# Logarithms, the first unit pair, the second modulation sums and two pairs of unit buffers moved in a two-block transformer kernel

## The reference, cut to what matters

```
mod = silu(c) @ w_ada + b_ada                 # sh1, sc1, g1, sh2, sc2, g2
h = rms_norm(x) * (1 + sc1) + sh1
z, xbc, dt, q, k, v = split(h @ w_in)
y_ssd = norm(ssd(silu(conv(xbc)), dt) * silu(z))     # 4 chunks of 128 tokens
y_sb: logits = q k^T * scale; log_rem = log_sigmoid(-logits) below the diagonal
      log_between = reversed cumulative sum of log_rem - log_rem
      weights = exp(log_sigmoid(logits) + log_between);  y_sb = weights v
x = x + g1 * (concat(y_ssd, y_sb) @ w_out)
x = x + g2 * swiglu(rms_norm(x) * (1 + sc2) + sh2)
```

## Time and profile before

| what | before |
|---|---|
| time, median of 3 runs | 2187.24 us (2186.93 to 2187.7) |
| profiled execution | 2188.19 us, span 2186.4 us |
| PE busy | 98%, 9964 matmuls |
| DVE busy | 1037.7 us (47%) |
| ACT busy | 750.0 us (34%) |
| POOL busy | 890.1 us (41%) |
| PEld busy | 1685.0 us (77%) |
| mean granted TensorE clock | 0.987 |

### The profile page before, as it was taken

How to read it: one execution, slowest core, us unless ns; L and a number is a source line. 1 busy time by engine, 2 the same in 40 slices (tenths; PEclk the granted TensorE clock), 3 DMA queues, 4 the chain that set the end, 5 groups by cost and what they waited for, 6 DMA issues and landing times.

```text
span 2186.4 us, 26047 instructions
## 1 busy us (share of the span) xinstructions
PE 2131.9 (98%) x9964; PEld 1685.0 (77%) x9964; DVE 1037.7 (47%) x1726; ACT 750.0 (34%) x1106; POOL 890.1 (41%) x717
## 2 busy tenths in 40 slices
PE   7999999999999999999999989999999998999999
PEld 5888888888888445888888867767778876888887
DVE  5445653562434895566256162655655644110111
ACT  4124321222223786322122243543454333222221
POOL 4445545454433211554455334222221243454444
PEclk9999999999999999999999989999999999999999
DMA  4223333422531000342442222111111122223222
GB/s 167 96 97 135 137 118 133 171 101 73 194 115 63 1 1 20 135 153 101 156 148 101 74 92 86 41 56 58 39 58 58 57 79 77 96 77 109 103 75 99
DMA packets 34204, 204.97 MB, mean 94 GB/s; under 512 B 4160, under 2 KB 5312, under 8 KB 14784
## 3 DMA queue, kind: packets, MB, share of 16 engines
q1 hardware_dynamic: 31968, 196.84, 25.6%
q10 hardware_dynamic: 2144, 6.88, 1.0%
HBM read 199.58 MB, written 2.10 MB: 92 GB/s over the span
## 4 chain that ended last, share of the span: by engine, by line
PE 68%; issue 14%; POOL 11%; DVE 4%; ACT 1%; DMA 0%; SPq 0%; POOLq 0%; DVEq 0%; ACTq 0%
PE PS L508 14%; PE PS L509 14%; PE PS L510 14%; POOL WL L446 11%; PE PS L599 4%; PE PS L601 3%; PE PS L600 3%; PE PS L777 2%; PE PS L790 2%; PE PS L808 2%; PE PS L958 1%; PE PS L926 1%; PE PS L920 1%; PE PS L1031 1%; PE PS L899 1%
## 5 line engine op out<-in xcount | busy, mean ns | idle before, releaser
L446 POOL TENSOR_TENSOR WL<-WR,WH 128x512 fp32r<-128x512 f32 (+2 forms) x692 | 858.5, 1271 | 1186.9 <-ACT WH L1152 1186.9
L508 PE MATMUL PS<-Hh,WH 128*128 128x512 f32 x1536 | 606.2, 395 | 22.9 <-DVE Hl L1679 9.8
L509 PE MATMUL PS<-Hl,WH 128*128 128x512 f32 x1536 | 601.3, 391 | 0.0
L510 PE MATMUL PS<-Hh,WL 128*128 128x512 f32 x1536 | 600.9, 391 | 0.0
L1152 ACT ACTIVATE WH<-WR 128x2048 fp32r<-128x2048 f32 (+2 forms) x173 | 305.9, 1768 | 702.3 <-PE PS L510 661.5
L508 PEld LDWEIGHTS PS<-Hh,WH 128*128 128x128 f32 x1536 | 290.6, 189 | 89.2 <-issue 14.6
L509 PEld LDWEIGHTS PS<-Hl,WH 128*128 128x128 f32 x1536 | 290.7, 189 | 62.2 <-issue 2.2
L510 PEld LDWEIGHTS PS<-Hh,WL 128*128 128x128 f32 x1536 | 290.5, 189 | 61.0
L508 PE MATMUL PS<-Gh,WH 128*128 128x512 f32 x592 | 232.2, 392 | 0.0
L509 PE MATMUL PS<-Gl,WH 128*128 128x512 f32 x592 | 232.0, 392 | 0.0
L510 PE MATMUL PS<-Gh,WL 128*128 128x512 f32 x592 | 231.7, 391 | 0.0
(11 more groups left out here) (279 smaller groups left out, 2372.6 us busy)
## 6 DMA issues: line engine op xcount, KB each, us to landing
WR<-wA SPq DMA_DIRECT2D x125, 1024.0 KB, 4.8
AW<-wada SPq DMA_DIRECT2D x24, 1024.0 KB, 6.8
WR<-wB SPq DMA_DIRECT2D x24, 768.0 KB, 4.1
WR<-wC SPq DMA_DIRECT2D x24, 640.0 KB, 3.9
X<-x_in SPq DMA_DIRECT2D x8, 256.0 KB, 6.5
W1K<-w1k ACTq DMA_DIRECT2D x1, 2048.0 KB, 8.0
W1V<-w1v ACTq DMA_DIRECT2D x1, 2048.0 KB, 12.9
out<-X SPq DMA_DIRECT2D x8, 256.0 KB, 4.8
```

Source lines behind the costliest of these rows:

```text
L446: ins = nc.gpsimd.tensor_tensor(WL[:, s, piece], WR[:, s, piece], WH[:, s, piece].bitcast(F32), ALU.subtract)
L508: nc.tensor.matmul(PS[:, b, :], wh[:, c, cols], pe_h, start=c == 0, stop=False)
L509: nc.tensor.matmul(PS[:, b, :], wh[:, c, cols], pe_l, start=False, stop=False)
L510: last = nc.tensor.matmul(PS[:, b, :], wl[:, c, cols], pe_h, start=False, stop=c == seg.chunks - 1)
```

## The change

It has six parts.
1. Own buffers (`WX`) for the high and low parts of the first two units of qkv and of gu2a, at addresses that are free then. Their high parts no longer wait for the tiles of unit u-2. In `dense_squares` ACT writes them before the squares of the last unit's tiles. POOL makes the low part of the first in one 128x2048 instruction (`first_low`), DVE that of the second (`low_of_unit`), in the residual of dn1b ahead of tile 7 and in that of woh ahead of tile 6. With `low_at`, the additions for tile 6 also stand ahead of tile 7.
2. The masks' copies, whose place the new buffers of qkv use, go behind qkv tile 5.
3. Start: ACT calls `hi(1)` behind the third square, and `hi(2)` behind the eighth; POOL signals each of unit 1's four pieces, PE waits piece by piece, and `norm_stats` stands behind unit 1's first tile.
4. `mod_sums(1)` goes from between gu1b and dn1b to the norm behind dn1b: 11 columns ahead of the sum of `ACCF`, 13 behind `norm_stats`, in bank 6. DVE adds its bias behind the norm's chunks.
5. Stick-breaking: ACT's logarithm 1 ahead of exponential 2, DVE's cap 2 ahead of halves 0.
6. Chunks: `low_y(1)` goes from the end of chunk 3 into `last_rows`, behind `gate_y(2)` and a residual tile of wog.

```diff
+        WX = {SEGS["qkv"].unit0: (at("WXH0", 60, [P, KMAX], F32R), at("WXL0", 80, [P, KMAX], F32R)),
+              SEGS["qkv"].unit0 + 1: (at("WXH1", 68, [P, KMAX], F32R), at("WXL1", 88, [P, KMAX], F32R)),
+              SEGS["gu2a"].unit0: (at("WXH2", 64, [P, KMAX], F32R), at("WXL2", 80, [P, KMAX], F32R)),
+              SEGS["gu2a"].unit0 + 1: (at("WXH3", 52, [P, KMAX], F32R), at("WXL3", 88, [P, KMAX], F32R))}
...
+            def first_low(u):
+
+                wh, wl = WX[u]
+                pool.wait_ge(hi_s, u + 1)
+                nc.gpsimd.tensor_tensor(wl[:, :], WR[:, u % 2, :], wh[:, :].bitcast(F32), ALU.subtract)\
+                    .then_inc(lo_s, 1)
...
-                    body(0, 1)
+                    pool.wait_ge(hi_s, 2)
+                    for j in range(4):
+                        piece = slice(j * KMAX // 4, (j + 1) * KMAX // 4)
+                        nc.gpsimd.tensor_tensor(WL[:, 1, piece], WR[:, 1, piece], WH[:, 1, piece].bitcast(F32),
+                                                ALU.subtract).then_inc(w1l_s if j < 3 else lo_s, 1)
...
-                            if stats and first and k == 0 and tiles[0] == 0:
+                            if stats and first and k == (seg.unit0 == 0) and tiles[0] == 0:
                                 norm_stats()
...
-                    if r == 1:
-                        mod_sums(l)
+                    if r == 1 and l == 0:
+                        mod_sums(0, 5, 0, 24)
...
+            mod_sums(1, 6, 0, 11)
             pe.wait_ge(ssf_s, DC)
             nc.tensor.matmul(PS[:, 5, :], ones[:, :], ACCF[:, :], start=True, stop=True).then_inc(meanf_t, 1)
             norm_stats()
+            mod_sums(1, 6, 11, 24)
...
                     act.wait_ge(raw_s[s], 16 * (u // 2 + s))
+                    if u in WX:
+                        nc.scalar.activation(WX[u][0][:, :], WR[:, s, :], ACT.Copy).then_inc(hi_s, 1)
+                        return
                     if u >= 2:
                         act.wait_ge(tile_s, TILES_AFTER[u - 2])
...
-                    if u < seg.units - 1:
+                    ahead = u < seg.units - 1 or seg.unit0 + u + 2 in WX
+                    if ahead:
                         hi(seg.unit0 + u + 2)
...
-            for m in range(DC):
+            for m in range(3):
                 square(m)
             hi(1)
+            for m in range(3, DC):
+                square(m)
+            hi(2)
...
                     logarithm(i5, 0)
+                    logarithm(i5, 1)
                     exponential(i5, 2)
-                    logarithm(i5, 1)
                     logarithm(i5, 2)
...
+            def low_of_unit(u):
+
+                wh, wl = WX[u]
+                dve.wait_ge(hi_s, u + 1)
+                dve.wait_ge(lo_s, u)
+                nc.vector.tensor_tensor(wl[:, :], WR[:, u % 2, :], wh[:, :].bitcast(F32), ALU.subtract)\
+                    .then_inc(lo_s, 1)
...
                 for m in range(DC):
+                    early = low_at is not None and m == DC - 1
+                    if early:
+                        finished(m - 1)
+                    if m == low_at:
+                        low_of_unit(seg.unit0 + seg.units + 1)
                     dve.wait_ge(tile_s, seg.tile0 + m + 1)
...
                     cap(i5, 1)
+                    cap(i5, 2)
                     halves(i5, 0)
-                    cap(i5, 2)
                     halves(i5, 1)
...
-                if c >= 2:
-                    low_y(c - 2)
+                if c == 2:
+                    low_y(0)
...
                 gate_y(2)
                 attention_part(5)
+                low_y(1)
                 norm_y(2)
                 low_y(2)
```

More of the change, by code:

```diff
@@ L486, in body @@
                         wl = WL[:, s, 0:seg.size].rearrange("p (c m) -> p c m", c=seg.chunks)
-                        in_pieces = seg.unit0 == 0 and first and k == 0
+                        in_pieces = seg.unit0 == 0 and first
+                        if isinstance(i, int) and seg.unit0 + seg.upb * i + k in WX:
+                            wh, wl = (x[:, :].rearrange("p (c m) -> p c m", c=seg.chunks)
+                                      for x in WX[seg.unit0 + seg.upb * i + k])
                         if not in_pieces:
@@ L1204, in dense_squares @@
                             gained_square(m)
-                    if u == seg.units - 1:
+                    if not ahead:
                         hi(seg.unit0 + u + 2)
@@ L1271, in _ @@
             nc.scalar.activation(CSIL[:, :], pcol("cond", 0, 8), ACT.Silu).then_inc(cs_s, 1)
-            for u in range(SEGS["win"].units):
+            for u in range(1, SEGS["win"].units):
                 hi(u + 2)
@@ L1738, in residual @@
                     ins.then_inc(evac_s, 1)
-                    if m:
+                    if m and not early:
                         finished(m - 1)
@@ L1777, in gate_rows, with modulation @@
                         body(i)
+            def modulation(l, bank):
+                dve.wait_ge(mod_sum, l + 1)
+                nc.vector.tensor_tensor(MOD[:, 24 * l:24 * l + 24], PS[:, bank, 0:24],
+                                        pcol("bada", 24 * l, 24), ALU.add).then_inc(mod_done, 1)
             def feed_forward(l, next_h=None, scale=None, both=False):
@@ L1790, in feed_forward @@
                     last = half == "b" and scaled
[L1791 to L1794, removed]
+                    if last and l == 0:
+                        modulation(0, 5)
                     residual(f"dn{l}{half}", scale, squares=last, next_h=next_h if last else None,
-                             both=both and last, ada=12 * l + 6 if with_ada else None)
+                             both=both and last, ada=12 * l + 6 if with_ada else None,
+                             low_at=DC - 1 if l == 1 and last else None)
             def modulation_unit(n, f):
@@ L2017, in normalize, with masks @@
                                                SR[n % 2][:, :], ALU.mult, ALU.mult).then_inc(qk_s, 1)
+            def masks():
+                dve.wait_ge(mask_s, 32)
+                for dst, src in ((IDR, ident[:, :]), (NTRIR, NTRI), (NONESR, NONES)):
+                    chain.mark(nc.vector.tensor_copy(dst[:, :], src))
+                nc.vector.tensor_copy(MASKR[:, :], MASK).then_inc(cst_s, 1)
+                chain.wait()
             def first_qkv():
@@ L2285, in _ @@
             last_rows()
-            residual("woh", lambda m: MOD[:, DS(16 + m, 1)])
+            residual("woh", lambda m: MOD[:, DS(16 + m, 1)], low_at=DC - 2)
+            dve.wait_ge(mod_done, 2)
             gain_of("norm2", 32)
```

32 lines of the change are left out of this document (18 added, 14 removed).

## The result

The changed kernel takes 2161.03 us, median of 4 runs (2160.08 to 2165.98), against 2187.09 (2186.93 to 2187.7). The ratio on record is 0.9869, 95% interval 0.9855 to 0.9884; these two medians alone give 0.9881. Forecast were 2159.6, range 2153 to 2168. The profiled execution took 2160.74 us, with a span of 2158.9 us and a mean granted clock of 0.991 (0.987 before). Beside the experiments the kernel before ran 27 times more, and took 2186.7 to 2194.4 us; in experiment 5, on another chip, the medians differ by 2192.04-2161.86 = 30.2 us. So 26.1 us is one reading of a gain of 26 to 30.

A forecast was written before the change was run, and what follows sets the result against it. TensorE, busy 2131.9 of 2186.4 us, was taken to bound the kernel. Terms 9.0+8.55+6.1+3.9+2.6-2.55 = 27.6 us, subtracted from the median 2187.24, gave 2159.6 us; range 2155 to 2165 for the likeliest case, 2153 to 2168 with three rivals.

The forecast's parts named there:

- Start: First unit pair: unit 1 starts earlier, trailing its pieces, and unit 2 begins at 33.3 instead of 42.3; gain 9.0 us.
- Rival A: Start stays slow: TensorE's waits in pieces keep the half clock, costing 4.8 us; 2164.4 us, chance 0.12.
- Second sums: Second modulation sums leave their place before dn1b: 6.0 us plus 2.55 of half clock behind them; gain 8.55 us.
- Norm after dn1b: Moved sums, thirteen pairs at half clock, end after the old restart; TensorE restarts 2.55 us later, bounds 0 to 5.
- the lock: Norm after dn1b: VectorE's two-SBUF-input additions wait for GpSimd's whole 128x2048 instruction; the norm would lose 0.3 us more.
- Rival C: Norm after dn1b: sums keep the clock up, restart 2.6 us earlier, no half clock behind; 2154.5 us, chance 0.08.
- Stick-breaking: New orders remove four of TensorE's six waits for SPL (7.3 us in all), two of 0.6 stay; gain 6.1 us.
- rival B: Stick-breaking's waits only move to the middle sums or fifth half, 6.1 us not gained; 2165.7 us, chance 0.12.
- Last chunk: Gating starts earlier, so the stall for squares goes (2.7 us) with most half clock behind it (1.2); gain 3.9 us.
- Norm after woh: Without GpSimd's low part beside XN and Hl, TensorE restarts at 1819.0 instead of 1821.58; gain 2.6 us.
- Rivals D and E: D: clock stays half after dn1b's norm, 2206.6 us, chance 0.02; E: late loads, sums' cost cancel gain, 2187, chance 0.02.

The follow-up runs named there:

- experiment 5: The changed kernel profiled and timed once more, unedited, on another chip (the run also called again): 2161.86 us, ratio 0.9869.
- start_back: Changed kernel with its start undone (eight squares ahead of unit 1's high part, no pieces, norm's sum behind unit 0): 2167.37 us, ratio 0.9902.
- sums_back: Changed kernel with the second modulation sums back between gu1b and dn1b, none in the norm: 2165.49 us, ratio 0.9890.
- log_back: Changed kernel with ScalarE's old stick-breaking order alone (exponential 2 ahead of logarithm 1), VectorE's caps as changed: 2157.82 us, ratio 0.9864.
- lowy_back: Changed kernel with low_y(1) back ahead of gate_y(2), at the end of the last chunk: 2165.67 us, ratio 0.9887.

## Why the prediction was right

The time was forecast within 1.4 us of 26, by a sum whose terms held, but for two errors that nearly cancelled: the norm behind dn1b came out 2.58 us better, and half clock elsewhere took 3.44 us more (1.80 ahead of gu1a, 1.64 in the stick-breaking). That these cancelled is luck. In the second profile they are otherwise: the norm term is -3.29 and 0.05 is lost ahead of gu1a, and the gain in span is 26.5.

**Start.** 9.04 us against 9.0, and start_back gives 8.4 to 8.8. Rival A (half clock stays) is out: the window shows 1.00.

**Second sums.** 6.01+2.58 = 8.59 against 8.55; in sums_back 8.59 too.

**Norm after dn1b.** This term was mis-sized: -2.55 forecast, +0.03 found. The working priced thirteen pairs at 0.425 us, since the window before stood at half; in the first profile they ran at 0.227 (2.96 us for 26 instructions, 5.54 in again). L1127 came 0.77 us later against my 0.6, or 0.9 by the lock; the lock has no part in it, as VectorE's new subtraction was held by the high part and not by the additions (it waited 0.20 us for it, 1.11 in again). So the sums at the full level were my bound and not my value; the profiles show both, five to five, and a term of half the size, with that spread, would have been the better one. Rival C asked for this, and for full clock behind it: the first profile shows the first half, a restart 2.6 us ahead of the forecast's, but 3.4 us of half clock lie behind the restart there, as in each of the five.

**Stick-breaking.** The waits fell from 7.3 to 1.2 us in two of 0.6, as forecast to the tenth: rival B is out. The stages shrank by 1.74+2.72 = 4.46 only, as the changed kernel's first profile had 10.2 us of half clock at round 2's start, where the kernel before had 3.4. In log_back, with the same waits as the changed kernel and no half clock there, round 2 alone is 7.27 us shorter than before: 5.4 for the waits that went (6.6 to 1.2) and 1.6 for the 3.4 us of half clock by the prediction's 0.47. My sum had no term for half clock that comes without an edit.

**Last chunk.** 4.57 against 3.9; my price for the half clock behind the stall (1.2) was low: lowy_back's 4.30 less its wait of 2.44 leaves 1.86.

**Norm after woh.** 2.58 against 2.6.

**Not in the sum.** The block of 24 pairs ahead of dn0b, which the change leaves alone, was followed by 6.8 us of half clock instead of 3.4: 1.6 us lost, and with 0.18 at wq the rest of the difference. Sum of the stages: 9.04-1.80+8.59+0.03+4.46+4.57+2.58 = 27.47, of 27.46 in the span.

Rivals D and E have nothing for them: half clock behind the dn1b norm lasts 3.4 us after, and again holds 13.7 in one stretch with the norm's own.

What stays open: what decides, from one execution to the next on one kernel, whether a given stretch falls to half. It wasn't isolated. Nor was the move of the masks' copies (part 2), which the sum put at nothing: no run puts them back.

## What to carry to other kernels

When half clock differs between two executions of one kernel, compare lengths of stages cut at the same matmuls: undisturbed stages repeat to 0.01 us, and a 2 us edit is plain there when the medians scatter by 6. Spread products of one column among wide matmuls rather than issuing a block of them, even one without idle time. And where two orders on two engines are changed together, put each back alone: here only VectorE's counted.

## What the runs showed of the hardware that was not expected

- The 24 pairs of one column ahead of dn0b leave no gap on TensorE, and half clock followed them in every profile that has them in one block (3.4 to 10.2 us); spread three by three it followed in neither of two. Two profiles are few.
- A GpSimd subtraction of 128x2048 in one instruction takes 4.62 us, against 5.03 for four pieces in the earlier trace rows and 5.94 for four beside VectorE's additions; VectorE's takes 2.29, as estimated.
- On one kernel, the norm behind dn1b took 11.40 or 14.72 us, and round 2 129.07, 130.6 or 133.65 over kernels whose work in it is alike; runs of the changed kernel alone lie up to 6 us apart (2160.1 to 2166.0).
